# The order of TensorE's work in a step of four attentions: value products moved ahead of scores and transposes

## Chip, cores, metric

The program runs on one core of one Trainium2 chip. The metric is the device time of one execution in microseconds (us), shorter being better.

## What is computed

Two blocks on a sequence of 1024 tokens of width 1024, all in float32. The first block is an mLSTM and Fourier mixer with 16 experts. The second block has two layers, and each layer has two attentions. The change concerns only these four attentions, which the kernel calls A, B (even layer), C and D (odd layer):

```python
# A: 4 heads, two score maps each, one weight map; keys of all chunks up to the query's
w = p[:, :, 0] - lam * p[:, :, 1]
return jnp.einsum("bhqk,bkhe->bqhe", w.astype(v.dtype), v)
# B: 8 heads of 64, causal, with a forget bias
# C: 8 heads of 64, keys of the query's block of 128 and the one before it, a sink per head
# D: 8 heads of 64, at most 5 blocks of keys, a bias by relative position
p = jax.nn.softmax(s, axis=-1)
return jnp.einsum("bhqk,bkhd->bqhd", p.astype(v.dtype), v)
```

Each attention is scores, a softmax over the keys, and the product of the weights with the values.

## The kernel before

The whole program is one hand-written stream of instructions for each engine, joined by counting semaphores. Every engine works through its own stream in order, so an instruction that waits holds up all that stands behind it on its engine. The attentions stand in the order A, B, C, D, with projections of 1024 tokens between them.

An attention is cut into 32 **pairs** (class `Attn`, line 53): 4 head groups c by 8 blocks b of 128 queries, the blocks taken as 7, 0, 6, 1, 5, 2, 4, 3. A pair covers two score maps (two heads, or the two maps of one head in A), and nk blocks of 128 keys: nk is b + 1 in A and B, at most 5 in D, at most 2 in C. Pairs with nk above 4 have their scores in two chunks, the others in one. A pair goes through five stations, and one **step** does one station of five different pairs (line 88):

```python
yield pick(i), pick(i - 1), pick(i - 2), pick(i - self.LAG), pick(i - self.LAG - 1), self.fins.get(i - self.LAG, [])
```

In step i these are called a, e, w, t and u (LAG is 3), so u = i - 4 is the pair whose weights were transposed in step i - 1:

- **Scores** of pair a: TensorE, `scores` (line 1465, matmuls of L1474, in B also a mask, L1478), into PSUM banks 0 to 3. VectorE then adds the bias, copies the scores to SBUF and takes the maximum (`maxima`, L2537).
- **Exponentials** of pair e: ScalarE, L1939.
- **Weights** of pair w: VectorE, reciprocal of the sums (L2556); in A also the difference of the two maps (L2563, L2564); in C a sink term (L2555, L2547).
- **Transposes** of pair t: TensorE, `transposes` (L1492 for the first four key blocks, into bank 4 or 7 in turn; L1498 for the rest, into bank 5). ScalarE copies the first part to SBUF (L1951), VectorE the rest (L2572). A has one such turn in a step, B, C and D two (one for each head).
- **Outputs** of pair u: TensorE, `outputs` (line 1501; L1512 in A; L1517 and L1521 in the others) multiplies the transposed weights with the values, into PSUM **bank 6, the same for every pair** (line 512). VectorE then scales the result and writes it to SBUF (`outputs`, L2583 in A; L2586 and L2587 in the others). TensorE's product of pair t waits for the copies of its own transposes, and for VectorE to have emptied bank 6 of the pair before it:

```python
if t:
    pe.wait_ge(S(name + "_o"), before(name + "_o") + t)
```

In A, every eighth pair ends a head group, and its step also has `finish` (L1535), which waits for a normalization by ScalarE and VectorE (L1959, L1962, L2592, L2594).

VectorE's own order in a step (lines 2607 to 2625) is: `maxima(a, 0)`, `weights(w)`, `empty(t, 0)` (the copy of bank 5), in C `sinks(a)`, then `maxima(a, 1)` where there is a second chunk, then `outputs(u)`, then `empty(t, 1)`. ScalarE's is: exponentials of the first map of e, copy of (t, 0), exponentials of the second map, copy of (t, 1). Neither is touched.

Of the kernel before, what the change touches and what calls it, by code (L numbers as in the profile page):

```python
# [95 lines left out]
def build(nc, a, out, scratch):  # L96
# [4 lines left out]
    def S(name):  # L101
        name = shared[name][0] if name in shared else name
        if name not in sems:
            sems[name] = ctx.enter_context(nc.semaphore(name))
        return sems[name]
# [12 lines left out]
    with ctx:  # L118
# [12 lines left out]
        def before(name):  # L131
            return shared[name][1] if name in shared else 0
# [377 lines left out]
        def outputs_of(t):  # L510

            return bank(6)
# [287 lines left out]
        def span(c):  # L800
            return slice(c * P, (c + 1) * P)
# [278 lines left out]
        def _(pe):  # L1080
# [380 lines left out]
            def attn_pe(name):  # L1461
# [3 lines left out]
                def scores(g, j):  # L1465
                    c, b, k0, nk = at.pairs[g]
                    q, n = at.chunk0[g] + j, min(4, nk - 4 * j) * P
                    if q >= 2:
                        pe.wait_ge(S(name + "_s"), before(name + "_s") + 2 * (q - 1))
                    diagonal = name == "B" and j == at.chunks[g] - 1  # L1470
                    k = (k0 + 4 * j) * P
                    for h in range(2):
                        row = slice(HD * h, HD * (h + 1))
                        mm = pe.matmul(bank(2 * (q % 2) + h)[:, 0:n], qT2[row, c, span(b)], kT2[row, 0 if name == "C" else c, k:k + n],  # L1474
                                       start=True, stop=not diagonal, skip_group_check=diagonal)
                    if diagonal:
                        for h in range(2):
                            mm = pe.matmul(bank(2 * (q % 2) + h)[:, n - P:n], identb[:], maskb[:, NH * P:NH * P + P], start=False, stop=True,  # L1478
                                           skip_group_check=True)
                    mm.then_inc(S(name + "_qk"), 1)  # L1480

                def transposes(t, h):
                    nk, i = at.pairs[t][3], at.turns[t, h]
                    if name == "A":
                        pe.wait_ge(S("A_w"), before("A_w") + t + 1)
                    else:
                        pe.wait_ge(S(name + "_e"), before(name + "_e") + 2 * t + h + 1)
                    sv = sbuf_of(name, t, h)
                    if i >= 2:
                        pe.wait_ge(S(name + "_wevA"), before(name + "_wevA") + i - 1)  # L1490
                    for k in range(min(4, nk)):
                        mm = pe.transpose(turned(i)[:, span(k)], sv[:, span(k)], ident[:])  # L1492
                    mm.then_inc(S(name + "_trA"), 1)
                    if nk > 4:
                        if at.wide0[i]:
                            pe.wait_ge(S(name + "_wevD"), before(name + "_wevD") + at.wide0[i])
                        for k in range(4, nk):
                            mm = pe.transpose(bank(5)[:, span(k - 4)], sv[:, span(k)], ident[:])  # L1498
                        mm.then_inc(S(name + "_trD"), 1)

                def outputs(t):
                    c, b, k0, nk = at.pairs[t]
                    i = at.turns[t, at.heads - 1]
                    pe.wait_ge(S(name + "_wevA"), before(name + "_wevA") + i + 1)
                    if nk > 4:
                        pe.wait_ge(S(name + "_wevD"), before(name + "_wevD") + at.wide0[i + 1])
                    if t:
                        pe.wait_ge(S(name + "_o"), before(name + "_o") + t)
                    o = outputs_of(t)
                    if name == "A":  # L1510
                        for k in range(nk):
                            mm = pe.matmul(o[:, 0:P], wT[t % 2][:, k, :], v2[:, k0 + k, span(c)], start=(k == 0), stop=(k == nk - 1))  # L1512
                    else:
                        r = 2 * (t % 4)
                        pe.wait_ge(S(name + "_w"), before(name + "_w") + t + 1)
                        for h in range(2):
                            pe.matmul(o[HD * h:HD * (h + 1), P:2 * P], rinv[:, r + h:r + h + 1].to_broadcast([P, HD]), ident[:],  # L1517
                                      start=True, stop=True, skip_group_check=True)
                        for k in range(nk):
                            for h in range(2):  # L1520
                                mm = pe.matmul(o[HD * h:HD * (h + 1), 0:P], v2h[name][:, k0 + k, h if name == "C" else 2 * c + h, :],  # L1521
                                               wT[(2 * t + h) % 4][:, k, :], start=(k == 0), stop=(k == nk - 1), skip_group_check=True)
                    mm.then_inc(S(name + "_pv"), 1)

                def finish(c):

                    i = at.turns["fin", c]
                    pe.wait_ge(S("A_on"), before("A_on") + c + 1)
                    ob = obuf[c % 2]
                    for m in range(2):  # L1530
                        side, n = (("_wevA", i - 1), ("_wevD", at.wide0[i]))[m]
                        if n > 0:
                            pe.wait_ge(S(name + side), before(name + side) + n)
                        for b in range(4):
                            mm = pe.transpose((bank(5) if m else turned(i))[:, span(b)], ob[:, 4 * m + b, :], ident[:])  # L1535
                        mm.then_inc(S(name + ("_trA", "_trD")[m]), 1)

                for a, _, _, t, u, fins in at.steps():
                    if a is not None:
                        scores(a, 0)  # L1540
                    if t is not None:
                        transposes(t, 0)
                    if a is not None and at.chunks[a] > 1:
                        scores(a, 1)
                    if u is not None:
                        outputs(u)
                    if t is not None and at.heads == 2:
                        transposes(t, 1)
                    for c in fins:
                        finish(c)  # L1550
# [35 lines left out]
            N3.transposes(pe, 0)  # L1586
            qk_pe("aq", "ak", then_v="av", norm=N3)
            attn_pe("A")

            for n in range(2):  # L1590
                mm = group(pe, bank(5 + n)[0:8, :], [(wbf[:, 8 * k:8 * k + 8], H2[0][:, k, n * HALF:(n + 1) * HALF]) for k in range(KT)])
            mm.then_inc(S("forget_mm"), 1)
            qk_pe("bq", "bk", then_v="bv")
            attn_pe("B")
            gates_pe(0)
            out_pe(0)
# [5 lines left out]

            qk_pe("cq", "ck", late=last_norms_pe)
            attn_pe("C")
            qk_pe("dq", "dk", then_v="dv")
            attn_pe("D")
# [1216 lines left out]
```

## Time and profile before

| | us |
|---|---|
| median of 3 runs | 3093.51 (3090.52 to 3095.23) |
| the profiled execution's own time | 3090.86 |
| its span | 3089.0 |
| attention A, first scores to last finish | 1809.6 to 1952.4 |
| attention B, first scores to last outputs | 2117.7 to 2256.2 |
| attention C | 2542.2 to 2618.4 |
| attention D | 2769.2 to 2887.7 |

The four attentions take 476.0 us of the span (142.8, 138.5, 76.2 and 118.5). An engine's busy time is the time in which it had at least one instruction under way. Times in a row of the timeline are the start, in us from the span's start, and the duration; instructions of one engine overlap a little, so the pace of an engine is read from start to start.

### The profile page before, as it was taken

The numbers are of one execution on the slowest core, as the hardware profiler recorded it, in microseconds if no ns is written. First come the engines' busy times: TensorE is split into PE (matmuls) and PEld (weight loads), VectorE is DVE, ScalarE is ACT, GpSimd is POOL, SyncE is SP. The second block draws the span as 40 slices with busy tenths as digits, with TensorE's granted clock in tenths as the row PEclk, the third lists the DMA queues.
The fourth block names the chain that finished last, engine by engine and source line by source line (L and its number), as shares of the span: only waits on it lengthen the run. The fifth ranks groups of instructions, "written<-read, shape, count | busy, mean of one in ns | idle before, by whom it ended". The sixth has DMA issues, their size and how long they took to land. (4 is left out here: it accounts for less than half of the span.)

```text
span 3089.0 us, 38275 instructions
## 1 busy us (share of the span) xinstructions
PE 2841.3 (92%) x14090; PEld 2078.3 (67%) x14098; DVE 1623.7 (53%) x3168; ACT 1329.4 (43%) x2465; POOL 162.2 (5%) x180
## 2 busy tenths in 40 slices
PE   7999999999992899999996998899999989989998
PEld 3448885788782666666655765576677775866777
DVE  1258553344456666666645558454642548536433
ACT  2242253232242555555526447543642548436422
POOL 0000000000000010111106000000000000000000
PEclk9999999999995899999998998999999999999999
DMA  9621020323425799999975200211022201100121
GB/s 358 198 48 55 28 83 1 109 82 109 152 103 184 259 358 366 362 360 364 368 231 146 61 21 8 55 28 42 15 65 99 96 14 36 48 18 18 56 82 55
DMA packets 177164, 396.99 MB, mean 129 GB/s; under 512 B 7269, under 2 KB 8325, under 8 KB 176497
## 3 DMA queue, kind: packets, MB, share of 16 engines
q1 hardware_dynamic: 159280, 331.37, 31.0%
q0 software_dynamic: 17584, 63.53, 6.3%
q8 instruction: 99, 1.62, 0.2%
q14 instruction: 57, 0.46, 0.1%
q10 hardware_dynamic: 144, 0.01, 0.0%
HBM read 359.17 MB, written 35.71 MB: 128 GB/s over the span
## 5 line engine op out<-in xcount | busy, mean ns | idle before, releaser
L770 PE MATMUL psum<-ring_r,kctx_r 128*128 128x512 f32 (+1 forms) x544 | 213.7, 393 | 0.0
L770 PE MATMUL psum<-ring_r,cols_r 128*128 128x512 f32 (+1 forms) x544 | 211.7, 389 | 0.0
L1939 ACT ACTIVATE ring<-ring,att 128x256 f32<-128x256 f32 (+7 forms) x256 | 173.2, 677 | 65.8 <-DVE att L2537 65.7
L1474 PE MATMUL psum<-wide 64*128 64x512 f32 (+2 forms) x704 | 157.3, 531 | 23.1 <-DVE att L2537 20.1
L2402 DVE TENSOR_TENSOR ring_r<-ring,pair_r 128x1024 fp32r<-128x1024 f32 x128 | 148.1, 1219 | 24.0 <-ACT pair_r L1834 24.0
L1357 PE MATMUL psum<-ring_r,wide_r 128*128 128x512 f32 x384 | 151.3, 394 | 0.0
L609 DVE TENSOR_TENSOR ring_r<-ring,ring_r 128x1024 fp32r<-128x1024 f32 x48 | 58.8, 1226 | 129.6 <-ACT ring_r L606 129.2
L1300 PE MATMUL psum<-small_r,ring_r 128*128 128x512 f32 x320 | 125.8, 393 | 0.8 <-DVE pair L2292 0.8
L1302 PE MATMUL psum<-small_r,ring_r 128*128 128x512 f32 x320 | 126.3, 395 | 0.0
L1834 ACT ACTIVATE pair_r<-ring 128x1024 fp32r<-128x1024 f32 x128 | 124.4, 1046 | 0.0
L1492 PEld LDWEIGHTS psum<-ident,ring 128*128 128x128 f32 x640 | 69.6, 144 | 78.2 <-issue 50.6
L1492 PE MATMUL psum<-ident,ring 128*128 128x128 f32 x640 | 119.2, 295 | 2.9 <-DVE ring L2564 2.9
L770 PEld LDWEIGHTS psum<-ring_r,kctx_r 128*128 128x128 f32 x544 | 104.6, 192 | 22.3
L770 PEld LDWEIGHTS psum<-ring_r,cols_r 128*128 128x128 f32 x544 | 102.7, 189 | 21.3
L294 PE MATMUL psum<-pair,wide 128*128 128x512 f32 x256 | 114.2, 599 | 2.9 <-DMA pair<-in_w_down 2.9
L769 PE MATMUL psum<-small_r,kctx_r 128*128 128x512 f32 (+1 forms) x240 | 100.2, 418 | 16.0 <-issue 7.7
L294 PE MATMUL psum<-hidden,wide 128*128 128x512 f32 x256 | 112.6, 592 | 1.0 <-DVE wide L2413 1.0
L769 PE MATMUL psum<-small_r,cols_r 128*128 128x512 f32 (+1 forms) x240 | 97.0, 404 | 15.2 <-DVE wide_r L738 13.9
L1356 PE MATMUL psum<-pair_r,wide_r 128*128 128x512 f32 x256 | 103.2, 403 | 7.0 <-DVE wide_r L2394 3.9
L1571 PE MATMUL psum<-wide_r,ring_r 128*128 128x512 f32 x256 | 101.5, 397 | 0.0
L1358 PE MATMUL psum<-pair_r,wide_r 128*128 128x512 f32 x256 | 101.4, 396 | 0.0
L1301 PE MATMUL psum<-hidden_r,ring_r 128*128 128x512 f32 x256 | 101.1, 395 | 0.0
(508 smaller groups left out, 6982.9 us busy)
## 6 DMA issues: line engine op xcount, KB each, us to landing
ring<-in_w_gate SPq DMA_DIRECT2D x64, 1024.0 KB, 9.4
ring<-in_w_up SPq DMA_DIRECT2D x32, 1024.0 KB, 10.2
hidden<-in_w_up SPq DMA_DIRECT2D x32, 1024.0 KB, 9.9
hidden<-in_w_down SPq DMA_DIRECT2D x32, 1024.0 KB, 7.6
pair<-in_w_down SPq DMA_DIRECT2D x32, 1024.0 KB, 7.7
ring<-in_w_ada SPq DMA_DIRECT2D x24, 1024.0 KB, 13.7
ring<-in_w_in SPq DMA_DIRECT2D x24, 1024.0 KB, 7.3
ring<-in_even_w_in SPq DMA_DIRECT2D x16, 1024.0 KB, 13.7
```

What stands on the lines that cost most here:

```text
L294: mm = pe.matmul(outp, l, r, start=(i == 0), stop=(i == len(pairs) - 1))
L769: self.eng.matmul(outp, XHIGH[b][:, k, :], whigh(key, k)[:, 0:wd], start=(k == 0), stop=False)
L770: self.eng.matmul(outp, XHIGH[b][:, k, :], low[:, k, 0:wd], start=False, stop=False)
L1300: pe.matmul(outp, w, high[:, j, :], start=(j == 0), stop=False)
L1302: mm = pe.matmul(outp, lows[:, k, span(c)], high[:, j, :], start=False, stop=(j == kn - 1))
L1356: pe.matmul(outp, xh[:, k, :], high, start=(k == 0), stop=False)
L1357: pe.matmul(outp, xh[:, k, :], low[:, k, :], start=False, stop=False)
L1474: mm = pe.matmul(bank(2 * (q % 2) + h)[:, 0:n], qT2[row, c, span(b)], kT2[row, 0 if name == "C" else c, k:k + n], start=True, stop=not dia ...
L1492: mm = pe.transpose(turned(i)[:, span(k)], sv[:, span(k)], ident[:])
L1834: act.activation(MHIGH[j % 2][p // 2][:, PK * (p % 2):PK * (p % 2 + 1), :], MRAW[slot][:, ks, :], ACT.Copy).then_inc(S("mw_high"), 1)
L1939: act.activation(sv, sv, ACT.Exp, bias=nmx[:, q:q + 1], scale=-1.0, accum_out=esum[:, r:r + 1]).then_inc(S(name + "_e"), 1)
L2402: dve.tensor_tensor(MLOW[slot][:, ks, :], MRAW[slot][:, ks, :], MHIGH[j % 2][p // 2][:, PK * (p % 2):PK * (p % 2 + 1), :].bitcast(F32), AL ...
```

## The change

In each step TensorE does `outputs(u)` first, ahead of `scores(a, 0)`, where it stood behind `scores(a, 1)` and ahead of the second head's transposes. The same call is made, with the same waits; no other engine's order changes.

```diff
                 for a, _, _, t, u, fins in at.steps():
+                    if u is not None:
+                        outputs(u)
                     if a is not None:
                         scores(a, 0)
                     if t is not None:
                         transposes(t, 0)
                     if a is not None and at.chunks[a] > 1:
                         scores(a, 1)
-                    if u is not None:
-                        outputs(u)
                     if t is not None and at.heads == 2:
                         transposes(t, 1)
                     for c in fins:
```

## Rows read from the trace of the kernel before

**Rows 1.** The page: busy time and share of the span of each engine.
```profile
PE 2841.3 (92%) x14090; PEld 2078.3 (67%) x14098; DVE 1623.7 (53%) x3168; ACT 1329.4 (43%) x2465; POOL 162.2 (5%) x180
```

**Rows 2.** Windows: steps 4 to 31 of A, B, C and D; length, busy times, granted clock.
```profile
1822.12:1935.50 113.38, 97.53 (x569) 62.03 (x568) 97.14 (x326) 77.92 (x205) 1.06 (x2) 0.92 0.03 10
2132.88:2246.14 113.26, 113.26 (x1089) 74.74 (x1089) 75.17 (x280) 69.09 (x169) 2.11 (x4) 1.00 0.06 20
2552.49:2611.55 59.06, 59.06 (x538) 36.35 (x537) 49.15 (x256) 50.13 (x200) 0.00 (x0) 0.99 0.01 2
2782.73:2877.85 95.12, 95.12 (x899) 62.61 (x899) 63.70 (x280) 65.29 (x170) 2.14 (x4) 1.00 0.05 15
```

**Rows 3.** Timeline of attention C, steps 22 and 23, TensorE, VectorE and ScalarE.
```profile
2590.55 0.70 PE L1474 MATMUL psum<-wide 64*128 64x256 f32 x4
...
2591.40 0.48 DVE L2537 CUSTOM_DVE_ANT_0 ring<-psum,ctx_hidden,att 128x256 f32<-128x256 f32 x1
2591.55 0.44 PE L1517 MATMUL psum<-ident,att 128*64 128x128 f32 x4
...
2592.36 0.44 PE L1492 MATMUL psum<-ident,ring 128*128 128x128 f32 x2
...
2592.73 0.70 PE L1474 MATMUL psum<-wide 64*128 64x256 f32 x4
...
2592.84 0.38 ACT L1951 ACTIVATE small<-psum 128x256 f32<-128x256 f32 x1 [0.21 <-PE psum L1492]
2593.06 0.29 DVE L2587 TENSOR_TENSOR pair<-psum,small 128x128 f32<-128x128 f32 x1
...
2593.58 0.48 DVE L2537 CUSTOM_DVE_ANT_0 ring<-psum,ctx_hidden,att 128x256 f32<-128x256 f32 x1 [0.23 <-PE psum L1474]
```

**Rows 4.** Timeline of attention A, step 20 and the start of step 21.
```profile
1882.04 1.13 PE L1474 MATMUL psum<-wide 64*128 64x512 f32 x4
...
1883.32 0.69 DVE L2537 CUSTOM_DVE_ANT_0 ring<-psum,cols 128x512 f32<-128x512 f32 x1 [0.16 <-issue]
...
1883.99 2.05 PE L1512 MATMUL psum<-small,kctx 128*128 128x128 f32 x16
...
1885.97 0.92 PE L1474 MATMUL psum<-wide 64*128 64x384 f32 x4
...
1886.92 0.35 DVE L2583 TENSOR_SCALAR small<-psum,att 128x128 f32<-128x128 f32 x1
```

**Rows 5.** Timeline of attention A, step 17: a value product that waits for bank 6.
```profile
1873.88 0.35 DVE L2583 TENSOR_SCALAR small<-psum,att 128x128 f32<-128x128 f32 x1
...
1874.37 0.91 PE L1512 MATMUL psum<-small,sel_wT 128*128 128x128 f32 x6 [0.55 <-DVE small L2583]
```

**Rows 6.** Windows of rows 2 again, L1512 alone (A), then L1521 alone (B, C, D).
```profile
1822.12:1935.50 113.38, 35.99 (x252) 31.36 (x252) 0.92 0.03 10
...
2132.88:2246.14 113.26, 32.27 (x504) 28.48 (x504) 1.00 0.06 20
2552.49:2611.55 59.06, 16.11 (x208) 12.33 (x208) 0.99 0.01 2
2782.73:2877.85 95.12, 27.25 (x412) 23.46 (x412) 1.00 0.05 15
```

**Rows 7.** Windows around changes of the granted clock; the columns of rows 2.
```profile
1854.20:1857.60 3.40, 0.84 (x8) 0.60 (x6) 2.44 (x12) 3.36 (x9) 0.00 (x0) 1.00 0.00 0
1857.60:1864.40 6.80, 5.86 (x22) 3.07 (x21) 4.34 (x15) 4.53 (x12) 0.00 (x0) 0.51 0.00 0
...
2072.70:2079.50 6.80, 3.76 (x19) 2.92 (x18) 2.86 (x3) 3.08 (x5) 0.00 (x0) 1.00 0.00 1
```

**Rows 8.** Timeline of attention D, step 3, TensorE: transposes ahead of the clock's rise.
```profile
2779.24 1.23 PE L1474 MATMUL psum<-wide 64*128 64x256 f32 x4 [1.10 <-DVE att L2537]
2780.40 1.12 PE L1492 MATMUL psum<-ident,ring 128*128 128x128 f32 x4
...
2782.73 0.70 PE L1474 MATMUL psum<-wide 64*128 64x512 f32 x2
```

## The prediction

> **What bounds the kernel now.** I read the page first, then the windows of the four attentions, then the timeline of single steps. By the page TensorE is busy 92% of the span, and VectorE 53% [rows 1]: the reader is to see that a stall of TensorE costs time almost anywhere. The windows show this for the changed code. From step 4 to step 31 of B, C and D TensorE is busy for the whole stretch (113.26 of 113.26 us, 59.06 of 59.06, 95.12 of 95.12), while VectorE works 75.17, 49.15 and 63.70 us of it and ScalarE 69.09, 50.13 and 65.29 [rows 2]. In A TensorE is busy 97.53 of 113.38 us and VectorE 97.14, so there both are close to the limit. The three engines overlap because TensorE is never sent to wait for something just made: in a step of C the value product of pair u starts 1.00 us after the first scores of the step (2591.55 against 2590.55) [rows 3], and what it waits for has come meanwhile.
>
> **The change, part by part.** No instruction is added or removed, and no DMA moves; the product of pair u and its waits move ahead of up to two chunks of scores and one turn of transposes. A product waits for three things, and I ask of each when it is ready at its new place.
>
> First, the copy of its own transposes. The second head's transposes end step 22 of C at 2592.36 + 0.44 = 2592.80; ScalarE's copy runs from 2592.84 to 2593.22, and the next step begins at 2592.73 [rows 3]. The product would be 0.5 us too early.
>
> Second, bank 6. VectorE empties it of pair u - 1 until 2593.06 + 0.29 = 2593.35 [rows 3], 0.62 us after the step's begin; with the wake seen in A (the emptying ends at 1873.88 + 0.35 = 1874.23, the product starts at 1874.37, so 0.15 us [rows 5]) that makes 0.8 us. This is what the old trace shows, but it is not what the new kernel will find, because this wait closes a loop. In VectorE's order, `outputs(u - 1)` stands behind `maxima` of the same step, and these wait for that step's scores. Up to now those scores stood ahead of the product; now they stand behind it. So: product of u, then scores of a, then all of VectorE's work of the step up to the emptying of bank 6, and only then the next product. TensorE's product and first scores no longer overlap VectorE's work. Behind the waiting product stand all of TensorE's scores and transposes, and behind these wait VectorE's maxima and ScalarE's exponentials.
>
> The loop in C, from rows 3: the product issues for 2592.36 - 2591.55 = 0.81 us; scores to the first maximum, 2593.58 - 2592.73 = 0.85; VectorE from the first maximum to the end of the emptying, 2591.40 to 2593.35 = 1.95; wake 0.15. That is 3.76 us for a step that takes 2592.73 - 2590.55 = 2.18 now, or 1.58 more. The transposes lie beside VectorE's part, and ScalarE's copy too. In A, step 20 [rows 4]: product 1885.97 - 1883.99 = 1.98, first scores 1.13 - 0.07 = 1.06 (the overlap of 0.07 is that of the product, 2.05 against 1.98) and 0.22 to the first maximum (as in C: 0.85 less the 0.63 that scores issue for), VectorE from 1883.32 without a hole to 1886.92 + 0.35 = 1887.27, which is 3.95, wake 0.15: 7.36 us against 1885.97 - 1882.04 = 3.93 now.
>
> Third, VectorE's copy of bank 5 for pairs with nk above 4. In B and D it stands behind the emptying of bank 6 in the same step, so it belongs to the same stretch of VectorE, and the loop closes through it instead.
>
> Thus for every step the new length is about: issue time of the product + issue time of the first scores + VectorE's work of the step + 0.37 (0.22 and 0.15). I sum over the 28 steps in which both a and u exist [rows 2, 6]; that is a sum of issue and busy times, and where another wait ends last it is a little short. Products: in A 35.99 less 28 times 0.07 (that overlap) = 34.0; in B, C and D the time of L1521 and 0.20 for the L1517 ahead of each (my estimate: of its 0.44 in rows 3 the rest lies beside L1521), so 37.9, 21.7 and 32.9. First scores: by key blocks 0.42, 0.63, 0.85 and 1.06 for 1 to 4 blocks (0.63 and 1.06 from rows 3 and 4, the others in proportion), and in B 0.21 more for the mask of one-chunk pairs: 25.2 in A and D, 28.1 in B, 16.9 in C.
>
> - A: 34.0 + 25.2 + 97.1 + 10.4 = 166.7, against 113.4: 53 more.
> - B: 37.9 + 28.1 + 75.2 + 10.4 = 151.6, against 113.3: 38 more.
> - C: 21.7 + 16.9 + 49.2 + 10.4 = 98.2, and 5.4 for VectorE's own holes of 0.19 in each step (1.95 in the loop above against 49.15 / 28 = 1.76 busy), 103.6 against 59.1: 45 more.
> - D: 32.9 + 25.2 + 63.7 + 10.4 = 132.2, against 95.1: 37 more.
>
> The last four steps of each attention have no scores; there only the first wait counts, 0.5 us each: 8. The first four steps have no product and cost nothing. Sum so far: 181 us.
>
> **The clock.** In A the granted clock falls to 1.2 GHz after TensorE was busy 0.84 of 3.4 us, and stays there for the next 6.8 although it is busy 5.86 of them [rows 7]. It did not fall when TensorE was busy 3.76 of 6.8 us [rows 7]. In the new loop TensorE works 59.1 of 103.6 us in C (57%), 75% in B, 72% in D, with holes of about 1.6 us; I expect it to stay at 2.4 GHz, near the edge in C. In A it works 97.5 of 166.7 us (58%) with holes up to about 3 us (step 20 has 3.93 of work in 7.36), alternating with dense stretches; I expect falls again and again, about half of the stage at 1.2 GHz. There the product and the first scores take twice their time: up to 34.0 + 25.2 = 59 for the whole stage, so I take 25 (of the bounds 0 and 59, in the middle), and 5 more for B, C and D, which all begin at the low clock and must first come out of it. Together 30.
>
> The Trainium skill ("TensorE: Matmul & The Clock Gate", Part 4: PE-mode transpose) says that a transpose does not count as busy for the clock in the same way. Here the clock had risen by 2782.73, where the scores are back at their fast pace, after 2.3 us of nothing but transposes behind 1.2 us of scores [rows 8], so in this trace they seem to count. By that rule the counted work in C would be only 1.44 of 3.76 us, and the time that of rival 2.
>
> **Total.** 3090.9 (the profiled execution's own time) + 181 + 30 = 3302; the median of the runs shown lies 2.6 us above that execution, so **3305 us**.
>
> **Rivals.**
> 1. Only the lateness that the old trace shows is paid, without the loop: 0.6 to 0.8 us in a step of B, C and D and 1.45 in A (bank 6 empty at 1887.27, the next step begun at 1885.97 [rows 4], and the wake). 84 x 0.7 + 28 x 1.45 = 99: 3193 us. For it: the rows show just this. Against: VectorE's order is fixed, and its maxima cannot start ahead of the scores. 6%.
> 2. The loop is right, and the clock falls in B, C and D as well. Product and scores there make 66.0 + 38.6 + 58.1 = 163 us, which would double: half of the time at the low clock gives 82 more, 3387 us; all of it, 3468. For it: C's 57%. Against: the stretch at 2072.70 in [rows 7]. 16%.
> 3. Faster: TensorE waits 113.38 - 97.53 = 15.9 us in A [rows 2], in part for data of which VectorE gets its last piece later than it could. An earlier product lets VectorE empty bank 6 earlier, and if each product found its data ready, at best those 16 us would come back: 3078. This decides if copies and bank 6 are ready before the previous step ends; rows 3 have them 0.5 and 0.6 us behind. 2%.
> 4. The change does nothing, since some other wait already orders the engines so: then TensorE could not be busy 100% in rows 2. 1%.
>
> My forecast, the loop with falls of the clock in A alone, has 75%, and its own range is 3265 to 3350: 3262 would be no clock term and 0.10 instead of 0.15 for the wake; A all at 1.2 GHz gives 3340. The range for 8 in 10 reaches into rival 2: 3258 to 3385. A difference of 0.2%, 6 us, is about what a measurement of this kernel can tell from none. Faster 2%, within it 1%, slower 97%.
>
> **What would show it.** In the new profile the windows of B, C and D should have VectorE's busy time as before in a stretch longer by 34%, 75% and 39%; a step of C should be 3.7 to 3.8 us. L1512 and L1517 should wait for L2583 and L2587 (in B and D in part for L2572 or L1951), by 1.4 to 1.8 us a step in B, C and D and 2 to 3 us in A. VectorE's waits for L1521 and L1512 should be all but gone, replaced by waits for L1474. Outside the attentions nothing should change. A step of C near 2.9 us would mean rival 1. A low granted clock in C would be rival 2.

## The result

| | before | after |
|---|---|---|
| median, us | 3092.7 (4 runs, 3090.5 to 3095.2) | 3338.4 (4 runs, 3326.8 to 3340.2) |
| the profiled execution's own time | 3090.9 | 3340.2 |
| attention A, first scores to last finish | 142.8 | 214.4 |
| attention B | 138.5 | 191.5 |
| attention C | 76.2 | 154.6 |
| attention D | 118.5 | 167.3 |

The new order is slower by the ratio 1.078 (95% interval 1.076 to 1.081), 246 us, where 212 were forecast. The four attentions grew by 71.6, 53.0, 78.4 and 48.8, in sum 251.8 us; the spans differ by 249.4, so nothing outside them was lost.

The page after, engines and granted clock in 40 slices, against [rows 1]:

```profile
PE 2923.6 (88%) x14090; PEld 2135.3 (64%) x14098; DVE 1619.8 (49%) x3168; ACT 1327.5 (40%) x2465; POOL 161.0 (5%) x180
...
PEclk9999999999968999999798889989999956999999
```

VectorE and ScalarE do the same work in the same time. TensorE's same instructions take 82 us more busy time: they ran at a slower clock. In the last row each digit is a slice of 83 us; the 5 and the 6 eighth and seventh from the end are attention C.

The windows from the first product to the 29th (steps 4 to 31) of A, B, C and D after, against [rows 2]; the columns are length, busy times of TensorE, its weight loads, VectorE, ScalarE and GpSimd, granted clock, DMA:

```profile
1823.26:2003.67 180.41, 118.61 (x568) 76.86 (x569) 97.49 (x326) 77.90 (x202) 1.06 (x2) 0.82 0.02 6
2204.87:2368.80 163.93, 125.35 (x1089) 83.78 (x1089) 73.69 (x281) 69.82 (x168) 2.10 (x4) 0.92 0.05 14
2676.31:2808.47 132.16, 91.94 (x537) 59.03 (x537) 49.16 (x254) 47.16 (x198) 0.00 (x0) 0.58 0.00 1
2984.42:3126.35 141.93, 106.79 (x898) 69.06 (x898) 61.28 (x281) 64.52 (x169) 2.13 (x4) 0.93 0.03 10
```

VectorE's busy time is as before within 4%, in stretches longer by 67, 51, 73 and 47 us. TensorE, without a hole before in B, C and D, now has holes of 39, 40 and 35 us. And C stands out by its clock: a mean of 0.58 between the levels 0.5 (1.2 GHz) and 1 (2.4 GHz) means that 84% of it ran at 1.2 GHz.

One step of C in the timeline after, at 1.2 GHz, against [rows 3]:

```profile
2705.99 0.70 PE L1517 MATMUL psum<-ident,att 128*64 128x128 f32 x4 [1.39 <-ACT sel_wT L1951]
...
2707.47 1.23 PE L1474 MATMUL psum<-wide 64*128 64x256 f32 x4
...
2708.84 0.48 DVE L2537 CUSTOM_DVE_ANT_0 ring<-psum,ctx_hidden,att 128x256 f32<-128x256 f32 x1 [2.95 <-PE psum L1474]
...
2710.11 0.37 ACT L1951 ACTIVATE small<-psum 128x256 f32<-128x256 f32 x1
...
2710.64 0.29 DVE L2587 TENSOR_TENSOR pair<-psum,small 128x128 f32<-128x128 f32 x1
...
2711.03 0.69 PE L1517 MATMUL psum<-ident,att 128*64 128x128 f32 x4 [1.29 <-ACT small L1951]
```

The loop can be followed line by line: product at 2705.99, scores at 2707.47, VectorE's first maximum at 2708.84 after 2.95 us of waiting for them, bank 6 empty at 2710.64 + 0.29 = 2710.93, next product at 2711.03. The step takes 5.04 us where it took 2.18. The row puts the product's wait down to ScalarE's copy, but that ended at 2710.48, 0.55 us earlier; what came last is VectorE's L2587. VectorE's part, 2708.84 to 2710.93, is 2.09 us here; 0.23 of it waits for ScalarE's exponential of the sinks, which at this clock comes late. The same loop in one of the few stretches of C at 2.4 GHz:

```profile
2753.55 0.44 PE L1517 MATMUL psum<-ident,att 128*64 128x128 f32 x4 [1.60 <-ACT sel_wT L1951]
2754.36 0.70 PE L1474 MATMUL psum<-wide 64*128 64x256 f32 x4
...
2755.20 0.48 DVE L2537 CUSTOM_DVE_ANT_0 ring<-psum,ctx_hidden,att 128x256 f32<-128x256 f32 x1 [1.75 <-PE psum L1474]
...
2756.11 0.27 ACT L1951 ACTIVATE small<-psum 128x128 f32<-128x128 f32 x1
...
2756.68 0.29 DVE L2587 TENSOR_TENSOR pair<-psum,small 128x128 f32<-128x128 f32 x1
2757.07 0.44 PE L1517 MATMUL psum<-ident,att 128*64 128x128 f32 x4 [1.65 <-ACT small L1951]
```

That is 3.52 us: 0.81 + 0.84 + 1.77 (VectorE, 2755.20 to 2756.97) + 0.10. The prediction had 0.81 + 0.85 + 1.95 + 0.15 = 3.76.

In A the product's wait is named rightly. This releaser ended 62.4 of the 65.0 us that L1512's matmuls waited over the whole span (us, times):

```profile
  DVE small L2583: 62.4, 26
```

### The profile page after: what moved, and what is told of

Read it like the earlier page. It is cut to its first block and busy times, and to the rows that moved or that the text cites. A ratio compares the mean times of both kernels' runs of the same rounds, so it can differ in the third digit from the quotient of the medians.

```text
span 3338.4 us, 38275 instructions
## 1 busy us (share of the span) xinstructions
PE 2923.6 (88%) x14090; PEld 2135.3 (64%) x14098; DVE 1619.8 (49%) x3168; ACT 1327.5 (40%) x2465; POOL 161.0 (5%) x180
## 5 line engine op out<-in xcount | busy, mean ns | idle before, releaser
L1474 PE MATMUL psum<-wide 64*128 64x512 f32 (+2 forms) x704 | 181.5, 604 | 22.6 <-DVE att L2537 19.7
L1517 PE MATMUL psum<-ident,att 128*64 128x128 f32 x384 | 50.2, 341 | 115.3 <-ACT sel_wT L1951 38.4
L1492 PEld LDWEIGHTS psum<-ident,ring 128*128 128x128 f32 x640 | 88.1, 170 | 76.1 <-issue 71.8
L1492 PE MATMUL psum<-ident,ring 128*128 128x128 f32 x640 | 133.6, 337 | 0.5 <-DVE ring L2564 0.5
L1517 PEld LDWEIGHTS psum<-ident,att 128*64 128x64 f32 x384 | 23.9, 156 | 140.0 <-ACT small L1951 59.5
L1356 PE MATMUL psum<-pair_r,wide_r 128*128 128x512 f32 x256 | 103.2, 403 | 7.0 <-DVE wide_r L2394 3.9
L1474 PEld LDWEIGHTS psum<-wide 64*128 64x128 f32 x704 | 65.9, 225 | 62.9 <-issue 33.5
```

## The experiments

Ratios are against runs of the kernel before on the same chip. "Steps 4 to 31" is always the stretch of [rows 2].

**Where must the product stand?** Product behind the first scores, ahead of the transposes:

```diff
-                    if u is not None:
-                        outputs(u)
                     if a is not None:
                         scores(a, 0)
+                    if u is not None:
+                        outputs(u)
                     if t is not None:
                         transposes(t, 0)
```

> The product stands behind the first scores of the step, ahead of the transposes: the scores do not wait for it any more. Theory 1 (scores behind the product close the loop through VectorE; ScalarE's chain from the transposes through two copies back to the product stays): most of the loss is gone, C keeps about 0.8 us a step (22 us), B and D about 10 us each for the copy of the second turn, A 5 to 10; about 3145. Theory 2 (only the wait for bank 6 behind the scores matters): all is given back, 3093 to 3105. If neither loop were the cause but the mere lateness of the copies (0.5 us a step), the change from the new order would be small: above 3250.

Measured: 3150.9 us, ratio 1.018 (1.016 to 1.020). Moving two calls past each other gives back 188 of the 246 us, the low clock in B, C and D included: it is 1.00 there again. Windows of steps 4 to 31 of A, B, C and D:

```profile
1824.24:1940.98 116.74, 89.08 (x566) 63.06 (x565) 97.55 (x326) 77.09 (x199) 1.06 (x2) 0.94 0.03 10
2141.05:2266.53 125.48, 113.70 (x1086) 74.92 (x1084) 74.63 (x281) 68.70 (x167) 2.10 (x4) 1.00 0.05 18
2575.00:2658.77 83.77, 55.66 (x534) 36.73 (x533) 46.90 (x253) 47.02 (x198) 0.00 (x0) 1.00 0.01 1
2834.64:2937.61 102.97, 96.35 (x897) 63.30 (x895) 63.80 (x281) 63.94 (x169) 2.13 (x4) 1.00 0.04 14
```

Against [rows 2] that is 3.4, 12.2, 24.7 and 7.9 us more, where 5 to 10, 10, 22 and 10 were expected. So the loop that scores behind the product close through VectorE is three quarters of what the new order costs, and something else costs C 0.9 us a step. Its timeline shows it:

```profile
2619.89 0.44 PE L1517 MATMUL psum<-ident,att 128*64 128x128 f32 x4 [0.86 <-ACT small L1951]
...
2621.17 0.38 ACT L1951 ACTIVATE kctx<-psum 128x256 f32<-128x256 f32 x1 [1.35 <-PE psum L1492]
...
2621.45 0.50 ACT L1939 ACTIVATE ring<-ring,att 128x256 f32<-128x256 f32 x1
...
2621.94 0.19 ACT L1944 ACTIVATE att<-att 128x2 f32<-128x2 f32 x1
2622.03 0.37 ACT L1951 ACTIVATE sel_wT<-psum 128x256 f32<-128x256 f32 x1
2622.16 0.16 DVE L2547 TENSOR_TENSOR att<-att 128x2 f32<-128x2 f32 x1 [1.29 <-ACT att L1944]
...
2622.56 0.29 DVE L2587 TENSOR_TENSOR pair<-psum,small 128x128 f32<-128x128 f32 x1
...
2622.95 0.44 PE L1517 MATMUL psum<-ident,att 128*64 128x128 f32 x4 [0.97 <-ACT sel_wT L1951]
```

ScalarE waits 1.35 us for the first head's transposes, which stand behind the product, then copies them, and only then does the second exponential, the exponential of the sinks (L1944) and the second copy. That is a second chain, through ScalarE's order. The row puts the product's wait down to the second copy, but that ended at 2622.40, 0.55 us before the product. VectorE waited 1.29 us for L1944, and its emptying of bank 6 behind that ended at 2622.85, 0.10 before the product. So in C this chain runs: product, transposes, copy, exponential, sink, VectorE's sum with the sink, emptying of bank 6, product. The second copy is a branch beside it, which takes over where bank 6 is free earlier.

**Is the one output bank the whole loop?** New order, outputs of C in two banks:

```diff
-        def outputs_of(t):
+        def outputs_of(t, name=""):
 
-            return bank(6)
+            return bank(5) if name == "C" and t % 2 else bank(6)
...
-                    if t:
-                        pe.wait_ge(S(name + "_o"), before(name + "_o") + t)
-                    o = outputs_of(t)
+                    held = 2 if name == "C" else 1
+                    if t >= held:
+                        pe.wait_ge(S(name + "_o"), before(name + "_o") + t + 1 - held)
+                    o = outputs_of(t, name)
...
```

The cut at the end is VectorE's side, which reads the bank that TensorE wrote.

> New order; in attention C alone the outputs alternate between banks 6 and 5 (bank 5 is not otherwise used in C), so a product waits for the emptying of the pair two before it. Theory 1 (two chains: the one through VectorE's emptying of the bank, and right behind it one through ScalarE: transposes of the first head, copy, exponentials, copy of the second head, next product): in the changed kernel at the low clock the second head's copy ends 0.55 us before the product starts, in a step of 4.9 us, so only about 0.5 us a step comes back, C gets some 14 us shorter (of 132 us for steps 4 to 31), the clock stays low, and the time is about 3325. Theory 2 (the single output bank is the whole cause): C falls to TensorE's own work and 0.5 us for the copy, 2.7 us a step, some 55 us less: about 3283.

Measured: 3308.6 us (3287.8 to 3319.5), ratio 1.067 (1.062 to 1.072). Neither number was met. In the profiled execution the clock in C rose 34 us after step 4 began and stayed up, which I had not expected, and C took 97.5 us for steps 4 to 31. The step settles what the bank is worth. C at 2.4 GHz:

```profile
2746.70 0.44 PE L1518 MATMUL psum<-ident,att 128*64 128x128 f32 x4 [1.00 <-ACT small L1952]
...
2749.48 0.37 ACT L1952 ACTIVATE sel_wT<-psum 128x256 f32<-128x256 f32 x1
...
2749.90 0.44 PE L1518 MATMUL psum<-ident,att 128*64 128x128 f32 x4 [1.11 <-ACT sel_wT L1952]
```

A step takes 3.20 us, against 3.5 with one bank and 2.7 if the bank were all. The product now starts 0.05 us after the copy's end (2749.85): ScalarE's chain is right behind VectorE's.

**ScalarE's chain by itself.** Two banks in C as above, and in C both exponentials ahead of the first copy:

```diff
-                    if t is not None:
+                    if t is not None and not (name == "C"):
                         empty(t, 0)
                     if e is not None:
                         exponentials(e, (1,))
+                    if t is not None and name == "C":
+                        empty(t, 0)
```

> As the kernel with two output banks in C (product to product 3.20 us at 2.4 GHz there), and ScalarE in C does both exponentials of its step ahead of the first copy. Theory 1 (what remained was ScalarE's chain: copy of the first head, exponentials, sink, copy of the second head): only product, scores, both transposes, one copy and two hand-overs remain in a row, 0.81 + 0.63 + 0.37 + 0.44 + 0.48 = 2.7 us a step, steps 4 to 31 of C take 76 to 82 us instead of 97.5, clock at 2.4 GHz; about 3288. Theory 2 (the second copy waits for its transposes anyway): 3.2 us a step and no change, 3300 to 3310.

Measured: 3289.2 us, ratio 1.066 (1.064 to 1.068). Steps 4 to 31 of C:

```profile
2680.97:2757.63 76.66, 62.47 (x536) 39.81 (x536) 46.38 (x250) 47.25 (x197) 0.00 (x0) 0.90 0.01 1
```

76.7 us, 2.74 a step: theory 1, though not its clock. One step of it at 2.4 GHz:

```profile
2736.95 0.38 ACT L1952 ACTIVATE sel_wT<-psum 128x256 f32<-128x256 f32 x1
...
2737.39 0.44 PE L1518 MATMUL psum<-ident,att 128*64 128x128 f32 x4 [0.53 <-ACT sel_wT L1952]
...
2740.01 0.44 PE L1518 MATMUL psum<-ident,att 128*64 128x128 f32 x4 [0.53 <-ACT small L1952]
```

The times of this kernel and of the one with two banks alone overlap (3285.0 to 3298.7, 3287.8 to 3319.5), so the reading rests on the step: 2.62 us against 3.20, both at 2.4 GHz. With both chains gone C costs 17.6 us more than before, 0.63 a step, and some of that is 20% of the stretch at 1.2 GHz. The rest is the lateness of the last copy, 0.53 us in each of these steps, which is all that rival 1 of the prediction allowed for.

**VectorE's side of the loop.** New order, and VectorE empties bank 6 first in its step:

```diff
+                    if u is not None:
+                        outputs(u)
                     if a is not None:
                         maxima(a, 0)
...
                     if a is not None and at.chunks[a] > 1:
                         maxima(a, 1)
-                    if u is not None:
-                        outputs(u)
```

> New order on TensorE, and VectorE also does outputs(u) first in its step, ahead of maxima(a, 0). Theory 1 (the loop through bank 6 is closed by VectorE's order: emptying behind maxima): bank 6 is free early, the product then waits for ScalarE's copy or for VectorE's copy of bank 5, and 65 to 75 us come back: about 3268. Theory 2 (the product waits for the copies anyway, and VectorE, which now has to wait for the product before its maxima, only loses): 3338 or more.

Measured: 3225.8 us, ratio 1.043 (1.041 to 1.045), 113 us better than the new order alone: theory 1, and more than its 65 to 75, in part because the clock stayed up in B, C and D as well (1.00 in each). Steps 4 to 31 of A and C:

```profile
1825.26:1979.87 154.61, 113.68 (x568) 75.14 (x569) 97.43 (x324) 76.69 (x202) 1.06 (x2) 0.83 0.02 8
...
2628.41:2714.91 86.50, 56.26 (x536) 36.17 (x536) 51.23 (x252) 46.71 (x197) 0.00 (x0) 1.00 0.01 1
```

C is at 3.1 us a step, ScalarE's chain again: in the step that begins at 2683.77 the product starts 0.06 us after the second copy's end. A still loses 41 us, at a clock of 0.83. Its largest wait is now that of L1512 for VectorE's copy of bank 5 (L2572), 25.4 us in 11 waits; that copy stands behind the maxima.

**Both reorders**, VectorE's as above and ScalarE's in all attentions, with the new order:

> New order on TensorE; VectorE empties bank 6 first in its step, and ScalarE does both exponentials ahead of the first copy, in all four attentions. Theory 1 (two loops, each removed by its own reorder): against VectorE's reorder alone (3226) another 25 to 30 us, 20 of them in C (105 to about 87): about 3198. Theory 2 (ScalarE's order has no part in it): 3226.

Measured: 3197.2 us, ratio 1.036 (1.034 to 1.038). And ScalarE's with the product behind the first scores:

> The product behind the first scores and ahead of the transposes (3151 alone), and ScalarE does both exponentials ahead of the first copy. Theory 1 (of the 57 us that this place still costs, most in C is ScalarE's chain): C falls from 104 to 75 us, B and D lose 3 us each, A nothing: about 3115. Theory 2 (the rest is the lateness of the copies whatever ScalarE does first): 3151.

Measured: 3121.3 us, ratio 1.011 (1.009 to 1.012). Steps 4 to 31 of C there:

```profile
2577.49:2635.00 57.51, 55.20 (x535) 36.82 (x533) 47.25 (x254) 46.23 (x195) 0.00 (x0) 0.99 0.01 2
```

57.5 us against 59.1 before the change: in C the whole loss is gone. Both kernels came out as theory 1 said (3198 and 3115), the second 6 us above it: in A the reorder cost 3 us instead of nothing, and C gained 26 us instead of 29. What the second kernel still loses, 30 us, lies in A, B and D; its causes were not separated.

**The clock in C.** New order, with eight transposes of the identity into the unused bank 5 at the end of each of C's steps, which nothing reads:

```diff
                     if t is not None and at.heads == 2:
                         transposes(t, 1)
+                    if name == "C" and u is not None:
+                        for k in range(8):
+                            pe.transpose(bank(5)[:, 0:P], ident[:], ident[:])
```

> New order; in attention C alone TensorE does eight more transposes of the identity matrix into the unused bank 5 at the end of each step (0.9 us at 2.4 GHz), which nothing reads: work that lies in the hole ahead of the product. Theory 1 (C was 30 us longer than the sum said because the clock stayed at 1.2 GHz, and it stayed there because TensorE idles 1.6 us in each step; transposes count as work for the clock): the clock rises, C's steps 4 to 31 take 28 x 3.55 = 99 to 105 us instead of 132, about 3308. Theory 2 (the length of C is not a matter of the clock, or transposes do not count): no gain; at the low clock the filler takes 1.8 us against a hole of 1.3, 5 to 15 us more, about 3348.

Measured: 3309.4 us, ratio 1.070 (1.068 to 1.072). Steps 4 to 31 of C:

```profile
2674.36:2775.61 101.25, 80.72 (x760) 61.42 (x761) 48.95 (x253) 47.20 (x198) 0.00 (x0) 1.00 0.01 2
```

More work on TensorE makes C 31 us shorter: 101.3 us at a granted clock of 1.00, where the loop's sum had said 103.6. So the sum for C was right, and its remainder is the clock. The filler is made of transposes alone (1.04 us a step; the trace lists them as MATMUL), and the mean clock is 1.00 instead of 0.58: the rule that the prediction cited from the Trainium skill ("TensorE: Matmul & The Clock Gate", Part 4), that these do not count in the same way, is not what this chip did here.

**Does C's clock come from C?** The new order in C alone:

```diff
+                first = name == "C"
                 for a, _, _, t, u, fins in at.steps():
-                    if u is not None:
+                    if u is not None and first:
                         outputs(u)
...
+                    if u is not None and not first:
+                        outputs(u)
                     if t is not None and at.heads == 2:
                         transposes(t, 1)
```

> The new order in attention C alone; A, B and D keep the old one. Theory 1 (each attention pays for itself, and the clock in C is low because of C's own holes and not of what came before): C again takes 145 to 160 us instead of 76, most of it at 1.2 GHz, and the time is 3093 + 70 to 84, about 3170. Theory 2 (the low clock of C comes from the stretches ahead of it): the clock rises at C's start as it did before, C takes about 120 us, about 3138.

Measured: 3160.6 us, ratio 1.023 (1.022 to 1.025). Steps 4 to 31 of C:

```profile
2553.00:2675.20 122.20, 80.35 (x537) 51.45 (x537) 49.12 (x254) 47.15 (x198) 0.00 (x0) 0.70 0.00 1
```

122.2 us at a mean clock of 0.70: C does it by itself, with A and B in the old order. It is 69 us more than before in all, a little under theory 1's 70 to 84, since the clock was low for less of C here (60%, against 84%). Why it was low for less was not tested.

**From the clock to a faster kernel.** In the old order the clock falls in A each of the three times that TensorE waits 2.6 us ahead of a finish while scores are still to come; [rows 7] has the first (a mean clock of 0.51 over the next 6.8 us), and behind the other two it is 0.71 and 0.79 over 3.4 us. Old order, with 20 transposes of the identity in that hole, into banks that the next scores overwrite:

```diff
+                    if name == "A" and fins and a is not None:
+                        q = at.chunk0[a + 1]
+                        pe.wait_ge(S(name + "_s"), before(name + "_s") + 2 * (q - 1))
+                        for k in range(20):
+                            pe.transpose(bank(2 * (q % 2))[:, 0:P], ident[:], ident[:])
                     if u is not None:
                         outputs(u)
```

> TensorE's old order; in attention A, in the three steps with a finish that still have scores to come, TensorE does 20 transposes of the identity matrix (2.2 us), read by nothing, into the banks of the next scores, ahead of the product that waits 2.56 us there for ScalarE. Theory 1 (this hole is what drops the clock for 6.8 us each time): the three falls at the finishes are gone, each gives back half of its 6.8 us where TensorE sets the pace, 5 to 10 us in all: about 3084. Theory 2 (the clock falls anyway after the second hole of 0.94 us, or the filler comes in the way): 3090 to 3096.

Measured: 3082.3 us, ratio 0.9967 (0.9955 to 0.9979): faster than the kernel before, by 10 us. A takes 135.9 us instead of 142.8; the profiled executions already differ by 2.1 us when A begins, so of the 10 us 7 are shown to be A's. The first of the three holes in the timeline, then a window over most of A:

```profile
1851.99 2.35 PE L1549 MATMUL psum<-ident 128*128 128x128 f32 x20
1854.73 0.49 PE L1512 MATMUL psum<-small,sel_wT 128*128 128x128 f32 x2 [0.39 <-ACT sel_wT L1956]
```

```profile
1822.00:1935.00 113.00, 101.34 (x669) 69.81 (x667) 99.80 (x335) 79.45 (x210) 1.06 (x2) 1.00 0.04 10
```

The wait is down to 0.39 us, and the clock is 1.00 where it was 0.92 in [rows 2]. ScalarE's reorder alone in the old order, and both edits together:

> TensorE's old order; ScalarE does both exponentials ahead of the first copy in all four attentions. Theory 1 (in the old order ScalarE's chain lies beside TensorE's work, which is busy without a hole in B, C and D): within 3 us of the kernel before, 3089 to 3095. Theory 2 (ScalarE's chain costs in the old order too): C more than 3 us shorter.

> Both of the edits of the two kernels beside it: ScalarE's exponentials first, and the filler in A. Theory 1: the two do not touch each other, the time is that of the filler alone, within 3 us: about 3084.

Measured: 3092.6 us, ratio 1.0002 (0.9992 to 1.0012), and 3084.2 us, ratio 0.9970 (0.9959 to 0.9980). In the old order ScalarE's chain lies wholly beside TensorE's work, as expected; the fastest kernels are the two with the filler in the old order, and they do not differ clearly.

## Why the prediction was right, and where it was not

- *The loop through bank 6.* Right, in its place and in its size at 2.4 GHz: 3.52 us measured for a step of C against 3.76, and 101.3 us against 103.6 for steps 4 to 31 with the clock held up. VectorE's part was too long by 0.18 us: in the step of [rows 3] it waits for ScalarE's exponential of the sinks, and at 2.4 GHz in the new loop that one is done in time.
- *The sums for B and D* (38 and 37 us) were too small: 50.7 and 46.8 measured, at clocks of 0.92 and 0.93. The prediction said that the sum falls short where another wait ends last; ScalarE's chain may be such a wait (it is shown in C alone), and by those clocks 16 and 14% of the stretches ran at 1.2 GHz, where the prediction had nearly none. How much is which was not separated.
- *A.* 67 us in steps 4 to 31, against 53 + 25 for the clock. The clock was lower for about a third of the time (a mean of 0.82), not for half of it.
- *The step that was mis-sized:* "I expect it to stay at 2.4 GHz, near the edge in C", and the 5 us for the clock in B, C and D. C lost 73 us in steps 4 to 31, 45 by the sum and 28 by the clock. That was rival 2 in one attention of three. The filler in C shows that the 28 are the clock's: with it up, the stretch took 101.3 us. Three windows of C after show when it changed:

```profile
2724.30:2731.10 6.80, 3.61 (x38) 2.40 (x37) 2.70 (x16) 3.08 (x14) 0.00 (x0) 1.00 0.00 1
2751.60:2758.40 6.80, 3.55 (x34) 2.13 (x33) 3.15 (x18) 3.23 (x14) 0.00 (x0) 1.00 0.00 0
2676.30:2724.30 48.00, 35.33 (x188) 22.23 (x188) 16.72 (x86) 15.67 (x67) 0.00 (x0) 0.50 0.00 1
```

  I had argued from one stretch with 3.76 us of work in 6.8 without a fall [rows 7]; here the clock fell after 3.61 and after 3.55 of 6.8. And I had not asked what brings it back: C begins at the low clock, as before the change, and here it stayed low for 48 us in which TensorE was busy 74% of the time (third row). It rose at 2724.3 and at 2751.6 behind denser pieces, 3.30 of 3.40 us busy and 3.18 of 3.40. A step at 1.2 GHz mostly has 3.7 us of work in 5.0 and no such piece.
- *Luck in the total.* 246 us against 212 is closer than the parts: in steps 4 to 31 A came out 11 us under its sum and clock term, while B, C and D came out 46 us over theirs (171 against 120 and 5), and the ends of the attentions cost 14 us instead of 8. The sums have two slips that decide nothing: by the prediction's own prices the first scores of the 28 steps add up to 25.6, 28.6, 17.0 and 25.6 us, not 25.2, 28.1, 16.9 and 25.2, and its low case without a clock term is 3269, not 3262.
- *Rival 1*, the mere lateness in the old trace, priced at 99 us, is refuted by the 188 us that one exchange of two calls gave back, and by the step of 3.52 us at 2.4 GHz, where it had 2.9. *Rival 3* and *no effect* are refuted by the result.
- *ScalarE's chain* was no step of the prediction, which had ScalarE's copy lie beside VectorE's part. In the new order it does, 0.55 us ahead of VectorE in the step shown; it sets the pace only where VectorE's loop is taken away.

What stays open: how the 22 us that B and D lost beyond their sums divide between other waits and the low clock, and how A's clock would behave with its holes filled in the new order. A second output bank was tried in C alone, since in A, B and D bank 5 takes transposes.

## What to carry to other kernels

When an operation is moved ahead in one engine's stream, its wait must be looked up in the other engine's order too: if what it waits for stands there behind work that needs what the operation was moved past, a loop closes, and the step becomes the sum of both engines' work. The lateness in the old trace (0.6 us here) then says little about the new one (1.3 us a step at full clock, 2.9 at half). Behind the loop that ends last there may be another nearly as long, so a second buffer alone can give back little (0.3 us of a step here, apart from the clock). And the engine that a wait is put down to in the trace must be compared with the end times: twice here it was the wrong one.

A stall of TensorE can have a second price, its clock; a filler that nothing reads, placed in the hole, shows in one run how much that is.

## What the runs showed of the hardware

- The granted clock does not follow TensorE's busy share alone. In the new order C stayed at 1.2 GHz for 84% of steps 4 to 31 with TensorE busy 70% of the time (91.94 of 132.16 us), while in the kernel with the product behind the first scores it stayed at 2.4 GHz with 66% (55.66 of 83.77).
- The kernel with two banks in C varies with its clock: four executions took 3287.8 to 3319.5 us, the shorter the higher their mean clock (0.949 for the shortest, 0.935 for the longest), while the kernel before stayed within 3090.4 to 3097.7 beside them.
- A filler of float32 transposes alone brought C from a mean clock of 0.58 to 1.00, and most of A from 0.92 to 1.00.
